# One pool of 16 row slots for the gathers of both expert tables

## What is computed

```python
def peer_ffn(xn, w_query, subkeys, u_tbl, v_tbl):      # for each chunk of 128 tokens
    q = (xc @ w_query).reshape(C, 8, 2, 128)
    s = einsum('chpd,hpnd->chpn', q, subkeys)
    s1, i1 = top_k(s[:, :, 0], 16);  s2, i2 = top_k(s[:, :, 1], 16)
    top_s, top_c = top_k((s1[..., None] + s2[..., None, :]).reshape(C, 8, 256), 16)
    idx = i1[top_c // 16] * 128 + i2[top_c % 16]
    act = gelu(einsum('chkd,cd->chk', u_tbl[idx], xc))
    coef = softmax(top_s) * act
    return einsum('chk,chkd->cd', coef, v_tbl[idx])
```

## Time and profile before

| | |
|---|---|
| three runs | 1693.29 us median (1691.18 to 1697.15) |
| the profiled execution | 1688.29 us, of it 1686.3 us span |
| mean granted TensorE clock | 0.879 |
| busy: PE, DVE, POOL, ACT | 1325.6, 1052.9, 988.3, 366.5 us |
| moved by DMA | 607.66 MB, of it 536.94 MB by the 1024 gathers |
| chain that ended last | PE 39%, DVE 16%, issue 14%, DMA 10%, POOL 10%, unknown queue 7% |

### The profile page before, as it was taken

One profiled execution on the slowest core, in us unless ns is written; L12 is line 12 of the kernel. 1 busy time (PEld: TensorE's weight loads), 2 busy tenths in 40 slices (PEclk: granted clock), 3 DMA queues, 4 the chain that ended last, 5 costly groups with the idle time before them and its releaser, 6 DMA issues.

```text
span 1686.3 us, 15100 instructions
## 1 busy us (share of the span) xinstructions
PE 1325.6 (79%) x4882; PEld 765.0 (45%) x4882; DVE 1052.9 (62%) x2495; ACT 366.5 (22%) x843; POOL 988.3 (59%) x1038
## 2 busy tenths in 40 slices
PE   9989788778768798849876899878987786665556
PEld 8976544344335454324543455535454442222222
DVE  3447477656766576655767845566667663866665
ACT  1111232112212223222212232133222221211101
POOL 0046466667666566646566765466666656666754
PEclk9989899889789898868898999889997988777778
DMA  9589999999999999999999999799999989899997
GB/s 333 178 302 339 359 340 358 375 391 382 381 368 355 342 401 406 399 408 404 385 404 378 360 400 404 293 397 328 373 406 365 349 299 385 323 365 368 377 334 301
DMA packets 197713, 607.66 MB, mean 360 GB/s; under 512 B 17597, under 2 KB 50437, under 8 KB 197637
## 3 DMA queue, kind: packets, MB, share of 16 engines
q0 software_dynamic: 147456, 536.94, 83.4%
q1 hardware_dynamic: 50048, 69.73, 11.9%
q10 hardware_dynamic: 132, 0.04, 0.0%
HBM read 605.59 MB, written 1.05 MB: 360 GB/s over the span
## 4 chain that ended last, share of the span: by engine, by line
PE 39%; DVE 16%; issue 14%; DMA 10%; POOL 10%; another core or an unknown queue 7%; ACT 3%; SPq 1%; POOLq 0%; DVEq 0%; ACTq 0%
PE sums L897 24%; POOL rows L654 10%; DVE rows L1707 8%; PE banks L754 8%; DMA rows<-in_peer_u,expert 6%; PE banks L771 4%; DMA rows<-in_peer_v,expert 3%; DVE h L1698 1%; DMA wring<-in_attn_w_q 1%; PE banks L780 1%; PE sums L763 1%; DMA h<-in_x 1%; DVE find L1606 1%; ACT soft_diag L1274 1%
## 5 line engine op out<-in xcount | busy, mean ns | idle before, releaser
L897 PE MATMUL sums<-rows,soft_diag 128*128 128x512 f32 x1764 | 865.4, 648 | 255.5 <-ACT soft_diag L1274 127.4
L654 POOL DMA_INDIRECT rows<-in_peer_v,expert x512 | 502.4, 981 | 448.8 <-PE sums L897 190.1
L1707 DVE SCALAR_TENSOR_TENSOR rows<-rows,xn_near 128x1024 f32<-128x1024 f32 x512 | 603.3, 1217 | 206.6 <-DMA rows<-in_peer_u,expert 176.6
L897 PEld LDWEIGHTS sums<-rows,soft_diag 128*128 128x128 f32 x1764 | 361.8, 209 | 727.7 <-issue 587.7
L654 POOL DMA_INDIRECT rows<-in_peer_u,expert x512 | 483.8, 945 | 235.8 <-issue 147.8
L1274 ACT ACTIVATE soft_diag<-ident,coef 128x128 f32<-128x128 f32 x446 | 138.4, 389 | 39.7 <-issue 22.6
L1266 ACT ACTIVATE gelu<-dots 128x8 f32<-128x8 f32 (+1 forms) x65 | 13.5, 208 | 582.7 <-DVE rows L1707 341.1
L1698 DVE SCALAR_TENSOR_TENSOR h<-rows,coef,h 128x1024 f32<-128x1024 f32 x63 | 80.7, 1281 | 0.0
L754 PE MATMUL banks<-xT,wring 128*128 128x128 f32 x512 | 65.0, 285 | 13.0 <-issue 10.6
L754 PEld LDWEIGHTS banks<-xT,wring 128*128 128x128 f32 x512 | 63.0, 201 | 18.0 <-issue 17.8
L1769 DVE SCALAR_TENSOR_TENSOR soft_diag<-banks,soft_diag 128x512 f32<-128x512 f32 (+1 forms) x8 | 7.7, 958 | 98.0 <-ACT soft_diag L1299 66.5
(11 more groups left out here) (209 smaller groups left out, 1019.7 us busy)
## 6 DMA issues: line engine op xcount, KB each, us to landing
wring<-in_w_kv SPq DMA_DIRECT2D x14, 1024.0 KB
rows<-in_peer_u,expert POOLq DMA_INDIRECT x512
rows<-in_peer_v,expert POOLq DMA_INDIRECT x512
wkept<-in_peer_w_query SPq DMA_DIRECT2D x8, 1024.0 KB
rows<-in_conv_w_in SPq DMA_DIRECT2D x7, 1024.0 KB, 11.9
wring<-in_peer_w_query SPq DMA_DIRECT2D x7, 1024.0 KB
wring<-in_attn_w_q SPq DMA_DIRECT2D x7, 1024.0 KB
wkept<-in_conv_w_out SPq DMA_DIRECT2D x4, 1024.0 KB
```

What stands on the lines that cost most here:

```text
L654: nc.gpsimd.indirect_dma_start(row[j], None, table, bass.IndirectOffsetOnAxis(ap=expert[n % 2][:, k:k + 1], axis=0)).then_inc(landed[j], 16)
L897: last = nc.tensor.matmul(sums[:, half, :], diag[:, k % GROUP, :], v_row[k % V_SLOTS][:, half * 512:(half + 1) * 512], start=(first and k ...
L1707: nc.vector.scalar_tensor_tensor(out=u_row[j], in0=u_row[j], scalar=1.0, in1=xn_near[:, :, :].rearrange("p a d -> p (a d)"), op0=ALU.mult, ...
```

## The change

The 16 slots become one pool. The slots are dealt out when the program is built, gather by gather in the order of issue: each gather takes the slot that is expected to be free first. A first-table row is taken to be done 8 gathers after its own (plus a little, to break ties), a second-table row 19 gathers after. The order of the gathers stays, and so does every instruction of every other engine; only the slot numbers and the semaphore that a gather waits for change, and `v_landed` becomes two semaphores a row, for even and odd groups, since rows of two groups can now be under way.

```diff
+    ROWS = U_SLOTS + V_SLOTS
+    row_slot, row_before = [], []
+    holder, free_at = [None] * ROWS, [0] * ROWS
+    for i in range(STEPS * GROUPS * ROWS):
+        slot = i if i < ROWS else min(range(ROWS), key=lambda s: (free_at[s], s))
+        row_slot.append(slot)
+        row_before.append(holder[slot])
+        holder[slot] = i
+        free_at[slot] = i + (8 + 0.1 * (i % ROWS) if i % ROWS < U_SLOTS else 19)
...
+            def wait_slot_free(i):
+
+                K, j = divmod(row_before[i], ROWS)
+                if j < U_SLOTS:
+                    pool.wait_ge(dot_done, GROUP * K + j + 1)
+                elif j < U_SLOTS + BY_PE:
+                    pool.wait_ge(v_used, BY_PE * K + j - U_SLOTS + 1)
+                else:
+                    pool.wait_ge(v_added, K + 1)
...
                 for j in range(GROUP):
-                    pool.wait_ge(dot_done, GROUP * (K - 1) + j + 1)
-                    gather(u_row, j, u_table, n, g * GROUP + j, u_landed)
+                    wait_slot_free(ROWS * K + j)
+                    gather(u_row(K, j), u_table, n, g * GROUP + j, u_landed[j])
                 for j in range(GROUP):
-                    if j < BY_PE:
-                        pool.wait_ge(v_used, BY_PE * (K - 1) + j + 1)
-                    else:
-                        pool.wait_ge(v_added, K)
-                    gather(v_row, j, v_table, n, g * GROUP + j, v_landed)
+                    wait_slot_free(ROWS * K + U_SLOTS + j)
+                    gather(v_row(K, j), v_table, n, g * GROUP + j, v_landed[j][K % 2])
```

More of the change, by code:

```diff
@@ L463, in trunk, with u_row, v_row @@
         rows = sb("rows", [P, U_SLOTS + V_SLOTS, D])
-        u_row = [rows[:, j, :] for j in range(U_SLOTS)]
-        v_row = [rows[:, U_SLOTS + j, :] for j in range(V_SLOTS)]
+        def u_row(K, j):
+            return rows[:, row_slot[ROWS * K + j], :]
+        def v_row(K, j):
+            return rows[:, row_slot[ROWS * K + U_SLOTS + j], :]
         flat = rows[:, :, :].rearrange("p s d -> p (s d)")
-        first_gain = v_row[6]
+        first_gain = v_row(0, 6)
         w_place = [wring[:, j] for j in range(W_RING)] + [
@@ L516, in trunk @@
         u_landed = [sem(f"u_landed{j}") for j in range(U_SLOTS)]
-        v_landed = [sem(f"v_landed{j}") for j in range(V_SLOTS)]
+        v_landed = [[sem(f"v_landed{j}_{odd}") for odd in range(2)] for j in range(V_SLOTS)]
         bank_done = sem("bank_done")
@@ L650, in early_weights_used, with gather @@
                     pool.sem_inc(slot_clear, 1)
-            def gather(row, j, table, n, k, landed):
+            def gather(row, table, n, k, landed):
                 nc.gpsimd.indirect_dma_start(
-                    row[j], None, table,
-                    bass.IndirectOffsetOnAxis(ap=expert[n % 2][:, k:k + 1], axis=0)).then_inc(landed[j], 16)
+                    row, None, table,
+                    bass.IndirectOffsetOnAxis(ap=expert[n % 2][:, k:k + 1], axis=0)).then_inc(landed, 16)
+            def wait_slot_free(i):
[6 more added lines that the diff above has]
+                    pool.wait_ge(v_added, K + 1)
             def first_group():
@@ L664, in first_group @@
                         early_weights_used(j)
-                    gather(u_row, j, u_table, 0, j, u_landed)
+                    gather(u_row(0, j), u_table, 0, j, u_landed[j])
                 for j in (6, 7, 0, 1, 2, 3, 4, 5):
@@ L671, in first_group @@
                         early_weights_used(U_SLOTS + j)
-                    gather(v_row, j, v_table, 0, j, v_landed)
+                    gather(v_row(0, j), v_table, 0, j, v_landed[j][0])
             def gather_group(n, g):
@@ L681, in gather_group @@
                 for j in range(GROUP):
-                    pool.wait_ge(dot_done, GROUP * (K - 1) + j + 1)
-                    gather(u_row, j, u_table, n, g * GROUP + j, u_landed)
+                    wait_slot_free(ROWS * K + j)
+                    gather(u_row(K, j), u_table, n, g * GROUP + j, u_landed[j])
                 for j in range(GROUP):
-                    if j < BY_PE:
-                        pool.wait_ge(v_used, BY_PE * (K - 1) + j + 1)
-                    else:
-                        pool.wait_ge(v_added, K)
-                    gather(v_row, j, v_table, n, g * GROUP + j, v_landed)
+                    wait_slot_free(ROWS * K + U_SLOTS + j)
+                    gather(v_row(K, j), v_table, n, g * GROUP + j, v_landed[j][K % 2])
             first_group()
+            assert all(before is None or i - before < 2 * ROWS for i, before in enumerate(row_before))
             for K in range(1, GROUPS * STEPS):
@@ L914, in combine_tail @@
                 pe.wait_ge(diag_ready, PE_ROWS * n + BY_PE + len(TAIL_PE) + 1)
-                pe.wait_ge(v_landed[k % V_SLOTS], 16 * (GROUPS * n + 2))
-                nc.tensor.matmul(sums[:, 1, :], diag[:, k % GROUP, :], v_row[k % V_SLOTS][:, 512:D],
+                wait_v_landed(pe, GROUPS * n + 1, k % V_SLOTS)
+                nc.tensor.matmul(sums[:, 1, :], diag[:, k % GROUP, :], v_row(GROUPS * n + 1, k % V_SLOTS)[:, 512:D],
                                  start=False, stop=True, skip_group_check=True).then_inc(v_used, 1)
@@ L1526, in _ @@
                 act.wait_ge(stream_ready, half + 1)
-                nc.scalar.activation(u_row[0][:, cols], h[:, 1, cols], ACT.Square, accum_out=stat[:, 0, half:half + 1]).then_inc(squares, 1)
+                nc.scalar.activation(u_row(GROUPS * STEPS - 1, U_SLOTS - 1)[:, cols], h[:, 1, cols], ACT.Square, accum_out=stat[:, 0, half:half + 1]).then_inc(squares, 1)
             act.wait_ge(means, normed_count("final", 1))
@@ L1706, in dot_group @@
                     dve.wait_ge(u_landed[j], 16 * (GROUPS * n + g + 1))
-                    nc.vector.scalar_tensor_tensor(out=u_row[j], in0=u_row[j], scalar=1.0,
+                    nc.vector.scalar_tensor_tensor(out=u_row(GROUPS * n + g, j), in0=u_row(GROUPS * n + g, j), scalar=1.0,
                                                    in1=xn_near[:, :, :].rearrange("p a d -> p (a d)"),
@@ L1920, in _ @@
                 j = k % V_SLOTS
-                dve.wait_ge(v_landed[j], 16 * (GROUPS * last + 2))
-                need(mark(nc.vector.scalar_tensor_tensor(out=h[:, 1, cols], in0=v_row[j][:, cols], scalar=coef[1][:, k:k + 1],
+                wait_v_landed(dve, GROUPS * last + 1, j)
+                need(mark(nc.vector.scalar_tensor_tensor(out=h[:, 1, cols], in0=v_row(GROUPS * last + 1, j)[:, cols], scalar=coef[1][:, k:k + 1],
                                                          in1=h[:, 1, cols], op0=ALU.mult, op1=ALU.add)))
```

14 lines of the change are left out of this document (8 added, 6 removed).

## The result

The changed kernel takes 1782.5 us in the median (4 runs), against 1695.2 for the kernel before: a ratio of 1.050, 95% interval 1.046 to 1.054, so some 85 us slower. The ratio leaves out one run of the changed kernel, 1822 us, that was in a slower state. I had forecast 1697 with a range up to 1724. The direction had a chance of 0.41; the size was far outside.

A forecast was written before the change was run, and what follows sets the result against it. POOL was taken as pacemaker, a gather each 1.24 us, held mostly by V-slot waits for PE. Terms + 20 - 12 - 7 - 5 + 8 = +4 us gave 1692 on the profile's scale, 1697 us as median; range 1674 to 1724.

The forecast's parts named there:

- Waits for PE fall by over 100 us, those for dots rise to 100 and more: Sign in POOL's waits in the changed profile: PE's down by over 100 us, dots' from 7.9 to 100 and more.
- TA' at the earliest TB + 17.0: Start of an even group's dots (TA') at least 17.0 us after the start of the preceding odd group's dots (TB).
- Gains of 12 us from 250 to 440: Four regular steps before the first mixer: POOL's stops shrink, 3.1 us a step in the mean, -12 us.
- Group 51, -7 us: Group 51, PE really late: U0 of 52 goes at 1387.4 in the place of 1394.56, -7 us once.
- V7's and PE's waits taken away bring something: V0 drops its wait for PE's first row, V7 its wait for the sum; gains counted as -12, -7 and -5 us.
- the mixer's steps, 480 to 1290, which I hold unchanged: Mixer's steps from 480 to 1290 us: held unchanged; a gain there would show the prediction wrong.
- the loss of + 20 us: Eight steps with even dots under 17.0 us behind odd ones, outside the DMA-bound stretch and DVE-late mixer steps: about +20 us.
- Behind an even group the search covers the same delay, so odd groups alone count: Even groups: the search (9 us and more) covers the added delay, so only odd groups' steps were priced.
- 8 us for late signals there: V0 of even groups, DVE's semaphore possibly late: 0.5 us a step in 16 steps outside the mixer, +8 us.
- The search is stretched: Rival: with POOL's stops gone at even groups, its running holds back others and lengthens searches; 1725 us, chance 0.17.
- Memory bounds it: Rival: DMA share 0.96 and more in nearly every stretch, so the change does nothing; 1693 us, chance 0.08.

The follow-up runs named there:

- Experiment 7: Kernel before plus V0's wait for its own group's first dot alone: 1798.6 us; plus five such dot waits in groups 16 to 50 alone: 1764.6 us.
- experiment 3: Kernel before with its own slots, plus waits of V0, V1, V2, V4, V6 for dots of their own group; nothing freed: 1796.4 us, ratio 1.0597.
- 8: Short POOL breaks (two memsets): kernel before, every eighth gather 1681.4 us, every fourth 1642.6 us; changed kernel, every eighth 1793.2 us.
- 9: Two-memset breaks at every fourth gather in the changed kernel: 1694.6 us; in the kernel before with V0's wait alone added: 1696.7 us.
- 5: Kernel before with half rows: gathers fetch 2 KB of a row in the place of 4 KB from group 1 on: 1681.9 us, ratio 0.9913.
- 11: Kernel before with half rows (2 KB gathers) and two-memset breaks at every fourth gather: 1642.3 us, ratio 0.9677.
- before_break4: Kernel before with a short POOL break (two memsets) ahead of U0, U4, V0 and V4 of every group: 1642.6 us, ratio 0.9721.

## Why the prediction was wrong

- *Waits for PE fall by over 100 us, those for dots rise to 100 and more*: right in kind (190.1 to 38.9, 7.9 to 349.7).
- *TA' at the earliest TB + 17.0*: right as a bound, and mis-sized by one us. From group 8 on no even group's first dot follows sooner than 18.0 us after the odd one's, where 12.5 was seen before. Experiment 7 confirms that V0 is the instruction that counts.
- *Gains of 12 us from 250 to 440*: not there. Group 8 to 10 takes 370.83 - 321.33 = 49.5 us in the place of 47.1 and not the 42.3 worked out. The odd part shrank as expected, from 21.8 to 18.0; the even part, which I had kept, grew from 25.3 to 31.5.
- *Group 51, -7 us*: a gain of that size came, but by luck. From the first dot of 51 to U0 of 52 it is 19.7 us in the place of 21.6, so 2 us of the 7; V3 goes 11 us behind V0, where 7 were worked out. From the first dot of 50 to that of 54 it takes 94.3 us in the place of 103.1, but since the search of the earlier trace rows fell from 24 to 9 us, which the sum did not have.
- *V7's and PE's waits taken away bring something*: 16 us in all by experiment 3 against the change, give or take 12, for 24 in the sum.
- **The failing step: "the mixer's steps, 480 to 1290, which I hold unchanged", and with it the loss of + 20 us.** I priced the added wait only by even groups with under 17 us behind odd ones, eight in all (six of them, some 12 us, in groups 16 to 50), and took DVE's lateness as room everywhere else. It is the other way: where DVE is late, POOL used to run ahead and used the time. In groups 16 to 50 V0 went before its group's first dot in 26 of 35 groups, 3.5 us ahead in the median and 11.2 at the most; after the change it goes 1.5 us behind it at the earliest, and V0 to V7 and the U rows behind them come after the late dot. The waits in groups 16 to 50 alone cost 63 us (7). The start, groups 1 to 7, was left out in the same way, and has 20 us.
- *Behind an even group the search covers the same delay, so odd groups alone count* (and 8 us for late signals there): wrong in the same way. After the change POOL is idle for 119 us ahead of V0 of even groups and for 183 us ahead of V0 of odd ones.
- *The search is stretched*: this rival had the right mechanism, and is now shown (8). It was mis-sized and misplaced: a price of 28 us in seven steps, in the search alone. Its share is about 40 us (9), and what grew with the change is DVE's idle time before softplus and gelu, behind PE's products and ACT's logs; the searches themselves are no longer in the mean than before (12.7 and 12.5 us). The argument against it, that V0's wait is a stop that frees the search, was wrong: V0's wait ends with the first dot, and then up to 16 gathers go at 1.24 us over the search that follows the dots.
- *Memory bounds it* (0.08): excluded twice (5, 11). The Trainium skill (SBUF — State Buffer, a bandwidth-pool intuition that's wrong, where the 358 GB/s of the prediction stand too) has HBM as the bound nearly always; these runs disagree, with 0.9913 for 44% fewer bytes.
- By the Trainium skill (SBUF — State Buffer, who interferes with whom) only GpSimd and VectorE can hold each other up, while TensorE and ScalarE never wait for anyone. The rows of L798 show TensorE slowed beside GpSimd's gathers too. The rule speaks of ports, and this is something else, or more.

What causes the slowing is open. The bytes are not it (13.1 us for the searches with half rows), nor is a long way to landing, by the same run, whose gathers landed in 2.7 us. Busy DMA engines alone are not it either: their share is as high in before_break4. What is shown is that it depends on the pace of issue. Whether it is the descriptors written, their signals or another shared path was not tried.

The traces hold a lead. Each gather reports its landing by 16 signals, and of these 16384 a trace keeps only a part: 40% in the kernel before, 34% with half rows, 36% after the change, but 70% in before_break4 and 77% with three memsets at every fourth gather. Signals are missing most where the slowing is worst. Two things follow. The names of who ended a wait, "remote" above all, rest on an incomplete list. And the recording itself may have a part in the slowing: every run here has a recorded span, so none can tell what breaks are worth without it.

## What to carry to other kernels

A wait put on the first of a row of in-order gathers costs the look-ahead of all behind it, and most where the engine waited for is late for reasons of its own. An engine that issues gathers and has time to spare can be tried at less than its full pace: here 0.7 us of idle work at every fourth gather made the kernel 2.8% faster than the one before, at 1642.6 us and, with half rows left aside, the best version of the study. DMA engines that are busy for 99% of a stretch prove no bound; halve the bytes and see.

## What the hardware showed

- Indirect gathers of 128 rows issued from GpSimd at 1.24 us each slow TensorE, VectorE and with them ScalarE's chain: matmuls 1.4 us apart in the place of 0.12, single VectorE instructions up to 3.9 us late, with "issue" or "remote" as the reason. This is so in recorded runs; there are no others here. At 1.42 us a gather nothing of it is left in the 31 searches.
- The gaps end some 3 to 6 us after the last gather (matmuls at 1232.04 after U7 at 1228.10; the search behind group 34 at about 1014 after 1008.57), about when its data has landed (last packets at 1234.2 and 1016.4).
- POOL's ownerless ("remote") waits go with its pace: 35 waits and 87.4 us at 1.24 us a gather, 1 wait and 2.2 us at 1.42.
